# A chunked RWKV-7 scan: four operands side by side in one buffer, turned by whole-array transposes, their next load asked for ahead of the last pair's store

## The reference

```python
def step(S, inp):
    r_t, w_t, k_t, v_t, kk_t, kka_t = inp
    sa = jnp.einsum("bhvk,bhk->bhv", S, kk_t)
    S = S * w_t[:, :, None, :] - sa[..., None] * kka_t[:, :, None, :] + v_t[..., None] * k_t[:, :, None, :]
    return S, jnp.einsum("bhvk,bhk->bhv", S, r_t)

s_final, ys = lax.scan(step, wkv0.astype(jnp.float32), xs)
```

## Time and profile before

| | |
|---|---|
| median of 3 runs | 4418.15 us |
| profiled execution | 4375.91 us |
| its span | 4374.1 us |
| PE busy | 3791.0 us (87%) |
| DVE busy | 3035.9 us (69%) |
| ACT busy | 958.0 us (22%) |
| POOL busy | 1802.3 us (41%) |
| granted TensorE clock, mean | 0.911 |

### The profile page before, as it was taken

The page is one execution under the profiler, slowest core; times in us unless marked ns, Lnnn a source line. Parts: engine busy times, 40 slices in busy tenths (PEclk is TensorE's granted clock), DMA queues, the critical chain, the costliest instruction groups (busy, mean ns, idle before and its releaser), DMA issues. The chain is left out here.

```text
span 4374.1 us, 71420 instructions
## 1 busy us (share of the span) xinstructions
PE 3791.0 (87%) x28135; PEld 2533.3 (58%) x28135; DVE 3035.9 (69%) x5964; ACT 958.0 (22%) x2001; POOL 1802.3 (41%) x1489
## 2 busy tenths in 40 slices
PE   7976878799999888888778886668999999999998
PEld 6766765655555488787565464564544544455444
DVE  0454431678588658777777488876989788977777
ACT  1331230110133322222451013780000000000001
POOL 0007000057223034433225207735666566666665
PEclk9997879899999998898789997669999999999999
DMA  7542254389577467766549633459999999999998
GB/s 176 164 157 92 83 187 171 112 338 410 210 261 255 175 232 240 259 221 211 207 137 382 242 144 49 97 147 404 406 411 390 403 403 409 379 410 413 413 412 325
DMA packets 390906, 1152.47 MB, mean 263 GB/s; under 512 B 78174, under 2 KB 148387, under 8 KB 372995
## 3 DMA queue, kind: packets, MB, share of 16 engines
q0 software_dynamic: 207216, 687.87, 43.2%
q1 hardware_dynamic: 150628, 419.97, 25.9%
q10 hardware_dynamic: 32727, 40.05, 2.6%
HBM read 1044.67 MB, written 113.65 MB: 265 GB/s over the span
## 5 line engine op out<-in xcount | busy, mean ns | idle before, releaser
L2793 PE MATMUL x_vps<-l_c_v,x_w 128*128 128x512 f32 x1536 | 676.6, 602 | 38.4 <-DVE x_w L2842 38.4
L2785 PE MATMUL x_sps<-c_big,l_c_wo 128*128 128x384 f32 x2048 | 671.8, 490 | 26.8 <-DMA l_c_wo<-u_cols 23.6
L387 POOL DMA_INDIRECT l_w_ring<-u_rows,k_eidx x256 | 297.5, 1162 | 908.4 <-DVE l_w_dots L443 366.8
L387 POOL DMA_INDIRECT w_ring<-u_rows,k_eidx x384 | 478.2, 1245 | 402.2 <-DVE w_dots L443 238.5
L2785 PEld LDWEIGHTS x_sps<-c_big,l_c_wo 128*128 128x128 f32 x2048 | 391.5, 192 | 307.6 <-DMA l_c_wo<-u_cols 31.7
L460 DVE SCALAR_TENSOR_TENSOR l_c_share<-w_ring,w_wts,l_c_share 128x1024 f32<-128x1024 f32 x384 | 493.6, 1285 | 93.8 <-DMA w_ring<-v_rows,k_eidx 81.6
L2793 PEld LDWEIGHTS x_vps<-l_c_v,x_w 128*128 128x128 f32 x1536 | 296.4, 193 | 412.7 <-issue 361.4
L387 POOL DMA_INDIRECT w_ring<-v_rows,k_eidx x384 | 411.6, 1072 | 159.3 <-issue 109.6
L387 POOL DMA_INDIRECT l_w_ring<-v_rows,k_eidx x256 | 289.8, 1132 | 328.8 <-DVE l_w_yacc L460 264.8
L460 DVE SCALAR_TENSOR_TENSOR l_w_yacc<-l_w_ring,l_w_wts,l_w_yacc 128x1024 f32<-128x1024 f32 x256 | 328.9, 1285 | 28.0 <-DMA l_w_ring<-v_rows,k_eidx 19.4
L443 DVE CUSTOM_DVE_ANT_0 w_ring<-w_ring,w_h 128x1024 f32<-128x1024 f32 x256 | 302.9, 1224 | 38.4 <-DMA w_ring<-u_rows,k_eidx 26.2
(11 more groups left out here) (652 smaller groups left out, 6282.3 us busy)
## 6 DMA issues: line engine op xcount, KB each, us to landing
l_c_wo<-u_cols SPq DMA_DIRECT2D x64, 1024.0 KB, 9.4
l_c_v<-v_rows SPq DMA_DIRECT2D x32, 2048.0 KB
e_c_w<-w_tiles SPq DMA_DIRECT2D x54, 512.0 KB, 3.6
l_c_w<-w_tiles SPq DMA_DIRECT2D x54, 512.0 KB, 6.8
l_c_wo<-s_G SPq DMA_DIRECT2D x16, 1536.0 KB, 9.2
s_rw<-l_q_out SPq DMA_DIRECT2D x48, 384.0 KB, 5.2
s_G<-l_c_share ACTq DMA_DIRECT2D x8, 2048.0 KB, 7.9
s_zT<-l_pz ACTq DMA_DIRECT2D x30, 384.0 KB, 7.1
```

The source lines that it names most:

```text
L387: pool.indirect_dma_start(out=self.ring[:, r, :], out_offset=None, in_=self.A[table], in_offset=bass.IndirectOffsetOnAxis(ap=idx[:, s:s + ...
L2785: mm = pe.matmul(sps[n % 2][:, 0:ND * P], u[n % 4][:, k, :], hT[:, k, :], start=(k == 0), stop=(k == KT - 1))
L2793: mm = pe.matmul(vps[k][:, x * 512:(x + 1) * 512], w[:, e, k * P:(k + 1) * P], v[:, e, x * 512:(x + 1) * 512], start=(c == 0 and e == 0), ...
```

## The change

The four operands that are turned (v, betae, kappae and a second copy of alpha) leave the two buffers, which now hold four operands each (`r_in0`, `r_in1`: alpha, beta, kappa, rho). They get one buffer for all pairs, in `sb_kept`. v lies on its lower 64 partitions and betae on its upper 64, kappae and alpha likewise behind them; for every chunk the 64 tokens of head 0 are followed by the 64 of head 1. So a load of one operand is two DMAs of 64 partitions, in runs of 64 numbers, and one `pe.transpose` of 64 partitions by 128 columns turns a chunk for both heads. The semaphore `rw_in` is one in place of two, and `load_turned(p)` waits for the batch an of pair p - 1, the last that reads the buffer.

```diff
-N_RW = 7
+N_RW, N_OP = 7, 4
...
-        rw = [kept[:, 0:N_RW * n].rearrange("p (i t) -> p i t", i=N_RW), sb("r_in1", [P, N_RW, n])]
+        by_token = [kept[:, i * n:(i + 2) * n].rearrange("p (c h t) -> p c h t", h=2, t=CL) for i in (0, 2)]
+        turn_from = {"vn": by_token[0][0:HD], "bn": by_token[0][HD:P], "kn": by_token[1][0:HD], "an": by_token[1][HD:P]}
+        rw = [sb(f"r_in{j}", [P, N_OP, n]) for j in range(2)]
...
-        FIRST_IN, THEN_IN = (R_ALPHA, R_BETA, R_KAPPA), (R_V, R_BETAE, R_KAPPAE)
+        FIRST_IN, THEN_IN = (R_ALPHA, R_BETA, R_KAPPA), (("vn", R_V), ("bn", R_BETAE), ("kn", R_KAPPAE), ("an", R_ALPHA))
...
                 for i in FIRST_IN:
                     sp.dma_start(rw[p % 2][:, i, :], A["rw"][p, i, :, tokens]).then_inc(ab_in[p % 2], 16)
-                for i in THEN_IN:
-                    sp.dma_start(rw[p % 2][:, i, :], A["rw"][p, i, :, tokens]).then_inc(rw_in[p % 2], 16)
+
+            def load_turned(p):
+                for name, i in THEN_IN:
+                    for h in range(2):
+                        sp.dma_start(turn_from[name][:, :, h, :], chunks(A["rw"][p, i, half(h), tokens])).then_inc(rw_in, 16)
...
             load_early(0)
+            load_turned(0)
             load_late(0)
...
             side.sp(sp)
+            sp.wait_ge(pe_prep, PP.after("an", 0))
+            load_turned(1)
             sp.wait_ge(pe_prep, PP.after("rkT", 0))
             load_early(2)
             for p in range(NPAIR):
                 if p + 1 < NPAIR:
                     bg.sp(sp, plan["turn"])
+                if p + 2 < NPAIR:
+                    sp.wait_ge(pe_prep, PP.after("an", p + 1))
+                    load_turned(p + 2)
                 if p:
                     store(p - 1)
                     load_gb(p)
...
                 if name == "vn":
-                    pe.wait_ge(rw_in[j], 48 * (p // 2 + 1))
+                    pe.wait_ge(rw_in, 32 * len(THEN_IN) * (p + 1))
...
                 for c in range(NC):
+                    if name in turn_from:
+                        rows = half(name in ("bn", "an"))
+                        mm = pe.transpose(ps[slot_of[name]][:, col(c)], turn_from[name][:, c].rearrange("f h t -> f (h t)"), ident[rows, rows])
+                        continue
                     for h in range(2):
-                        mm = pe.matmul(ps[slot_of[name]][half(h), col(c)], lhsT[half(h), col(c)],
-                                       ident[half(h), half(h)] if rhs is None else rhs[half(h), col(c)],
-                                       start=True, stop=True)
+                        mm = pe.matmul(ps[slot_of[name]][half(h), col(c)], lhsT[half(h), col(c)], rhs[half(h), col(c)], start=True, stop=True)
...
-            pool.wait_ge(rw_in[0], 48)
+            pool.wait_ge(rw_in, 32 * len(THEN_IN))
```

More of the change, by code:

```diff
@@ L1036, in attend_tiles @@
 def attend_tiles(A, pt):
-    o, out = (N_RW + 6) * pt.n if pt.first else 0, {}
+    o, out = (N_OP + 6) * pt.n if pt.first else 0, {}
     for name, dims in (("kT", (2, WIN + pt.n)), ("vT", (2, WIN + pt.n)), ("q0", (KT, WIN)), ("q1", (KT, WIN)),
@@ L1048, in kept_floats @@
     need = 2 * 2 * (WIN + pt.n) + 2 * KT * WIN + NH * 2 * WIN + NH + NB
-    return (N_RW + 6) * pt.n + need if pt.first else max((N_RW + 6) * pt.n, need)
+    return (N_OP + 6) * pt.n + need if pt.first else max((N_OP + 6) * pt.n, need)
 def load_attend(sp, A, pt, to, kv_sem, sem):
@@ L1119, in scan_pairs @@
         kept = A["sb_kept"]
-        part = lambda i: kept[:, (N_RW + i) * n:(N_RW + i + 1) * n]
-        rw = [kept[:, 0:N_RW * n].rearrange("p (i t) -> p i t", i=N_RW), sb("r_in1", [P, N_RW, n])]
+        part = lambda i: kept[:, (N_OP + i) * n:(N_OP + i + 1) * n]
+        by_token = [kept[:, i * n:(i + 2) * n].rearrange("p (c h t) -> p c h t", h=2, t=CL) for i in (0, 2)]
+        turn_from = {"vn": by_token[0][0:HD], "bn": by_token[0][HD:P], "kn": by_token[1][0:HD], "an": by_token[1][HD:P]}
+        rw = [sb(f"r_in{j}", [P, N_OP, n]) for j in range(2)]
         dend = two("r_dend", [P, NC])
@@ L1141, in scan_pairs @@
         const_in = sem("r_const_in")
-        ab_in, rw_in, rho_in, y_out = [[sem(f"r_{x}{j}") for j in range(2)] for x in ("ab_in", "rw_in", "rho_in", "y_out")]
+        ab_in, rho_in, y_out = [[sem(f"r_{x}{j}") for j in range(2)] for x in ("ab_in", "rho_in", "y_out")]
+        rw_in = sem("r_rw_in")
         att_in, kv_in, prm_in = sem("r_att_in"), sem("r_kv_in"), sem("r_prm_in")
@@ L1160, in scan_pairs @@
         tokens = slice(pt.t0, pt.t0 + n)
-        FIRST_IN, THEN_IN = (R_ALPHA, R_BETA, R_KAPPA), (R_V, R_BETAE, R_KAPPAE)
-        assert len({*FIRST_IN, *THEN_IN, R_RHO}) == N_RW
+        FIRST_IN, THEN_IN = (R_ALPHA, R_BETA, R_KAPPA), (("vn", R_V), ("bn", R_BETAE), ("kn", R_KAPPAE), ("an", R_ALPHA))
+        assert {*FIRST_IN, R_RHO} == set(range(N_OP)) and list(fill.values())[:4] == ["vn", "bn", "kn", "an"]
         def state(c, p, o):
@@ L1233, in prep_batch @@
                 name = order[g]
-                r = [rw[j][:, i, :] for i in range(N_RW)]
+                r = [rw[j][:, i, :] for i in range(N_OP)]
                 if name == "ab":
@@ L1249, in prep_batch @@
                     f"P{l}": (Pt[a], Pn[a], got), f"PT{l}": (Pn[a], Pt[a], got), f"X{l}": (Pn[b], X, (f"P{l}", f"X{l - 1}")),
-                    "vn": (r[R_V], None, ()), "bn": (r[R_BETAE], None, ()), "kn": (r[R_KAPPAE], None, ()), "an": (r[R_ALPHA], None, ()),
+                    "vn": (None, None, ()), "bn": (None, None, ()), "kn": (None, None, ()), "an": (None, None, ()),
                     "rbT": (r[R_BETA], r[R_RHO], ()), "rkT": (r[R_KAPPA], r[R_RHO], ()),
```

## The result

The changed kernel takes 4440.65 us (median of 6 runs, 4435.15 to 4450.09), the kernel before on the same chip 4416.61 us: ratio 1.006 (1.0044 to 1.0075), 24 us slower. The forecast was 4413 us, 5 us faster, in a range that ended at 4434.

The account below looks back on a forecast made before the run. PE (85% busy) was taken to lead most of a long turn, DVE (77%) its last chunks; POOL held DVE in short turns. -14.6 - 1 + 10.5 = -5 us on 4375.91, plus 42 us to the runs' median: 4413 us, range 4399 to 4434.

Parts of the forecast that it names:

- Transposes, -14.6 and -1: PE's four batches a turn: transposes at 57 ns each save 14.6 us in the long part, 1 us in the short.
- Rival 2: Transposes run like ordinary matmuls with 128 weight columns, 115 ns each: 10 us lost plus the stall, 4439 us; chance 0.13.
- rival 4: PE's clock falls in the long turns: one more 12 us low stretch a turn, 42 us in seven, 4455; chance 0.04.
- 213 ns for the lower clock: PE: the time a transpose with 128 weight and 128 moving columns would take at the lower clock, against 117 ns.
- Pair 1's stall, +10.5: Short part, turn 0: PE waits 26 us for pair 1's turned loads; turn 3 starts 10.5 us later.
- the two holds by POOL in turn 1: Short part: DVE operations held until POOL operations end, at 377.44 and 396.4, putting turn 2 at 414.0.
- DMAs of the long part: Eight turned loads a pair, 6.9 us of all engines, land before they are wanted: cost 0, up to 2 us a turn.
- 6 to 7 us for its eight issues: Long part: time SP needs to issue the eight turned loads ahead of the store, about the gap between two releases.
- The 18 ns for a packet of 256 B: Long part's turned loads: time per packet, so 6144 packets a pair need 6.9 us of all engines.
- Rival 3: DVE, busy 77%, sets the long turns' pace; only pair 0's batches pay: 4418 - 3 + 10.5 = 4426; chance 0.14.
- Rival 1: Short part: the stall is swallowed by the POOL stretch, +2 in place of +10.5 us: 4405; chance 0.22.
- rival 3 with the longer stall: Upper end of the forecast's range, 4434 us: DVE sets the long turns' pace and the short part's stall is longer.

Follow-up runs that it names:

- e1_matmuls: Changed kernel with the transposes alone undone: vn, bn, kn, an by two 64x64 matmuls a chunk, same 256 B loads; 1.0089 of before.
- e5_again: The changed kernel itself, unaltered, measured once more in another comparison; 1.0052 of before.
- e3_two: Changed kernel with a second buffer for the turned operands in the short part alone, pair 1's loads asked for ahead of the decode rows' loads; 1.0041 of before.
- e15_halves_at_an: Kernel before with v, betae, kappae in six loads of 64 rows, asked for after batch an, ahead of the store; 1.0064 of before.
- e2_runs: e1_matmuls with operands head by head in the buffer, so loads write runs of 3072 B (1024 B in the short part), not 256 B; 1.0084 of before.
- e9_alternate: e3_two with the eight turned loads in another order, the four of head 0 first, then those of head 1; 1.0020 of before.
- e17_long_behind: e9_alternate with the turned loads behind the store and gate and bonus in the long part alone; 1.0002 of before.
- e14_before_halves: Kernel before with v, betae, kappae in six loads of 64 rows for three of 128, same place, whole 3072 B runs; 1.0020 of before.
- e8_quiet: e3_two with the plain loads of alpha, beta, kappa moved to the next turn, after vn of the next pair; 1.0077 of before.
- e13_spread: e3_two with each operand's two turned loads asked for as soon as its own batch of the pair before is done; 1.0030 of before.
- e16_before_spread: Kernel before with v, betae, kappae each asked for after its own batch of the pair before, in plain loads of 128 rows; 1.0016 of before.
- e12_after_store: e3_two with the turned loads asked for behind the store and gate and bonus, in both parts; 1.0077 of before.
- e11_pairs_runs: 64x64 matmuls, 3072 B runs, second buffer in the short part, two operands a load: four loads of 128 partitions for eight of 64; 1.0495 of before.

## Why the prediction was wrong

Point by point:

- *Transposes, -14.6 and -1.* Right, though the interval of that gain is wide. 67 ns each for 57 and no dearer form of instruction; e1_matmuls against `e5_again` gives -16 us (-5 to -27), their long turns -13.7. Rival 2 is out, since they don't take 115 ns, and rival 4 as a cause: the clock falls in the windows of the stops, not at the transposes. The Trainium skill's rule on PE-mode transposes ("TensorE: Matmul & The Clock Gate", Part 4) would have put the fall on them; e1_matmuls, without any in the scan's preparation, has the same stops and is slower. (The forecast's 213 ns for the lower clock should be 2 x 117 = 234; nothing hangs on it.)
- *Pair 1's stall, +10.5.* The mechanism was right: 24.77 us of stall for 26. That turn 1 came at 367.4 for 367.5 is in part luck: turn 0 started 3.4 us late, the transposes at 349.1 for 347.0, and the rest of the turn took 18.3 us for the 20.2 laid out. The price was too high: turn 3 was late by 4.8 us, 3.4 of them from before turn 0, and e3_two gives back 5 (not told from nothing). The error is in the two holds by POOL in turn 1, which I added up to 414.0 and which came to 407.3.
- *DMAs of the long part, "Nothing waits; I cost it at 0".* This is the step that failed. It asked only whether the new loads are there by the time PE wants them. They are: PE waits for that buffer 0.2 us in the whole long part. But they cost some 35 us all the same (the 23 to 26 us of the result, plus the 16 us gained, less the 5 of the stall): the term priced the loads by their own deadline and not by what their packets hold up. What the runs show in its place: with these loads PE stands 28.5 us for 12.3 in the seven turns for want of instructions, and the rows' fetches wait longer too. e15_halves_at_an shows 28 us of the loss on the kernel before: 64-row loads and the place at 40 us of the turn, which together cost twice what they cost alone. The same term gave SP 6 to 7 us for its eight issues; they took 15.67.
- The 18 ns for a packet of 256 B were of packets elsewhere; here it was 24 to 29. The Trainium skill ("DMA: Bandwidth & Descriptors", Specifications) speaks against transfers under 512 B, and I cited it as harmless because no deadline was near. It was indeed not the cause: e2_runs with 3072 B is as slow as e1_matmuls with 256 B.
- *Rival 3* (DVE's pace) would have left the long turns as they were. They grew by 14 us at the same level. *Rival 1* (the stall swallowed, 4405) had the stall about right: its price was under the forecast's, but not the sign of the whole. In its range, rival 3 with the longer stall makes 4418 - 3 + 17 = 4432 and not 4434, which changes nothing.

What is shown: the place and the 64-row form of the loads carry most of the loss (e15_halves_at_an, 1.0064, against 1.0020 and 1.0012 for either alone), and PE's long stops end with the landing of a piece of its instructions (103 of 103). With the loads behind the store in the long part, a second buffer in the short one and the other order of loads, the changed kernel is level with before: 1.0052 to 1.0002, clear of the intervals. Of these three edits the place alone (e9_alternate to e17_long_behind, 0.0018) is inside them; what speaks for it are e14 to e15 in one comparison, and PE's issue stops, 8.4 to 15.0 us in the three versions with the loads behind the store and 25 or more ahead of it. What is argued: that the instruction pieces are late because of the loads' packets, which the versions' order fits and no run isolates, and how much of the 35 us is stops and how much is slower fetches of rows (POOL behind l_w_yacc 150.4 us for 132.2). Argued too is why the place matters: at 40 us of a turn PE leads at full clock with batches of the preparation, and a stop is lost; at 60 us DVE leads and PE runs at 0.50 in before's turn too, so it has time to spare. The losses of loads moved to 9 us of the turn (e8_quiet, of alpha, beta and kappa) or spread over it (e13_spread, e16_before_spread) fit that, and not a theory of the burst alone.

## What to carry to other kernels

A load that no one waits for is not free: ask at which point of the loop its packets fill the DMA engines, who leads there, and what else comes by DMA (instructions, gathered rows), and try it where the engine that sets the pace is waiting anyway. When an engine stops and no semaphore explains it, look at the queue of its instructions: it is in the same list of queues. A load that must be moved ahead for a short loop (22 us in e12_after_store) may be better behind in a long one with the same code. Price a stall and the gain of an instruction apart, as here, and then test the "costs nothing" line first, since it had no row behind it.

## What the runs showed of the hardware

- Loads of 64 partitions, whole rows of 3072 B: the same bytes take 2.1 us more of all engines in a turn than in loads of 128, and 14% of the packets take over 220 ns for 4%, at a median of 121 in both (e14_before_halves).
- A load whose source has an outermost dimension of 2 kept about 1.2 of 16 engines busy and held SP's queue for 14 to 26 us (e11_pairs_runs).
- A transpose of 32-bit numbers with 128 columns of weights and 64 moving ones takes 67 ns at full clock in a row of twelve.
- PE can stand up to 4.3 us (5.8 in e15_halves_at_an) in a stretch of full DMA engines with no semaphore to wait for, 28.5 us in seven turns for 12.3. Its instructions come in DMA packets of 16 KB, and each of the 103 stops of over 1.5 us in the long turns of all versions ends 1.2 to 1.9 us after such a packet.
- The same kernel has medians of 4373 to 4377 us in four comparisons and of 4417 and 4418 in two: a ratio within one comparison is worth more than two times from two.
